# A decoder kernel with nine row slots instead of ten, a resident weight block, and h turned by TensorE

## The chip, the core and the metric

The kernel runs on one core of one Trainium2 chip. The metric is the device time in microseconds, the median of several runs of the same program. The neighbouring cores do nothing.

## What is computed

A decoder trunk of two layers on 256 tokens of width 1024, all in 32-bit floats. Cut to what matters here:

```python
for l in range(2):                                   # DEPTH
    z = rmsnorm(x, g_mix[l]) @ w_in[l]               # zq, the keys and values, conv, pooling inputs
    x = x + concat([nsa(z), conv(z), pool(z)]) @ w_out[l]
    x = x + cross_attention(rmsnorm(x, g_xa[l]), rmsnorm(mem, g_mem[l]), ...)
    x = x + peer(rmsnorm(x, g_ffn[l]), ...)          # the experts
out = rmsnorm(x, final_g)

def peer(h, wq, sub_keys, u, v):                     # 8 heads x 16 experts of 16384 for each token
    expert_idx, gate = top16_of_pairs(top16(h @ wq, sub_keys))
    act = gelu(einsum('cd,chkd->chk', h, u[expert_idx]))
    return einsum('chk,chkd->cd', gate * act, v[expert_idx])
```

For each of the 256 tokens and in each layer, 128 experts are chosen by the data, and a row of `u` and one of `v` (1024 numbers each) are fetched for each of them.

`_pool_mixer` subtracts each value from its mean over the last 2, 4, 8 or 16 tokens.

## The kernel before

The tokens are worked on in two tiles of 128, one token in each partition. With two layers that makes four pieces of dense work (attention, convolution, pooling, cross-attention, choice of experts) and four pieces of experts' work. The program has five stages. Stage 0 does the dense work of layer 0, tile 0 alone. Stages 1 to 3 each do the experts' work of the piece before and the dense work of the next piece side by side. The last stage does the experts' work of the last piece and the final norm. A barrier of all engines stands between stages. In the profiled execution the stages start at 228.2, 655.6, 1060.3 and 1470.2 us; the prediction calls the one from 228 the second stage, the one from 655 the third and the one from 1060 the fourth.

**The experts' work.** 128 rows are gathered one after the other; "row" k is, for each of the 128 tokens, its k-th expert's `u` and `v`, 8 KB a partition. GpSimd issues the gathers (line 499) into `uv_rows`, which has `ROWS` slots, ten before (`ROWS = AHEAD * B` with `AHEAD` 5 and `B` 2). Before a gather it waits until TensorE has released the slot's last user (`slots_free`). After the gather it spreads the row's gate into a diagonal `diag` (line 493). VectorE takes the dot of the row's `u` half with h, held in PSUM as `h_ps` (line 540). ScalarE takes the gelu of two dots at a time (line 993) and multiplies it into `diag` (line 999). TensorE multiplies `diag` with the `v` half and adds into `acc_pe` (line 1265), and with that releases the slot. At the start of a stage VectorE copies `h_ffn` to `h_ps` (line 545). `h_ffn` is x times gain times 1/rms, made at line 845 in the step `ffn_norm`; the gain of 512 KB is loaded by SyncE for each stage (line 462).

**The dense work.** Each engine runs through the same written list of steps (`PLAN`, `MEM_PLAN`, `FIRST_PLAN`, `LAST_PLAN`). Between steps `run` lets it do as many pairs of rows as the table `TURNS` says, worked out once by `spread` from the steps' written lengths. So each engine's order is fixed, and an engine that waits in one step does none of the pairs behind it. The first steps of a stage are `mix_norm` (the norm on ScalarE and VectorE, then TensorE turns x) and `zq`, the first of the products with a weight block. VectorE has two dots ahead of the small instructions of `mix_norm`.

**The weight blocks.** The weights come in blocks of 16 KB a partition (2048 KB). SyncE loads them in the order of use into `w_ring`, which has two places (`RING`), and waits before each load until the last product with the block that holds the place is done. In stage 0 the slots of `uv_rows` are still empty, and three more places lie in them: ten slots minus the four that hold the memory tokens. `FIRST_PLACES` is the table of places of stage 0. Block `zq` of a layer is used in both of its tiles and is loaded in each.

**The rest.** `tcon` holds constants of a tile; its parts `cur` and `prev` are the pooling matrices, 4 x 128 columns each, multiplied in TensorE's step `turn_kv`. `h_t` holds the turned and gained activations that the products read.

Of the kernel before, what the change touches and what calls it, by code (L numbers as in the profile page):

```python
# [11 lines left out]
ALU = mybir.AluOpType  # L12
# [3 lines left out]
P = 128  # L16
# [24 lines left out]
B = 2  # L41
# [3 lines left out]
ROWS = AHEAD * B  # L45
# [21 lines left out]
for _name, _w in (("causal", S), ("cadd", NC), ("cvalid", NC), ("cur", 4 * P), ("prev", 4 * P), ("flag", 1)):  # L67
    TC[_name] = (_n, _w)
    _n += _w
# [37 lines left out]
FIRST_PLACES = [2, 3, 4, 0, 1] * 3 + [2, 0, 1, 0, 1]  # L107
# [79 lines left out]
for _bits in (10, 20):  # L187
# [6 lines left out]
    "tile_consts_loaded", "smalls_loaded", "fixed_loaded", "ident_loaded", "mem_loaded", "ffn_gain_loaded",  # L194
# [18 lines left out]
def build_program(nc, a):  # L213
    with ExitStack() as ctx:
# [8 lines left out]
        w_ring = sb("w_ring", [P, RING, KC * BLK])  # L223
        mem_k = sb("mem_k", [P, KC, N_MEM])
# [14 lines left out]
        pt_cmp = sb("pt_cmp", [P, P])  # L239
        h_ffn = sb("h_ffn", [P, D])  # L240
        hc = sb("hc", [P, 2, HIST + P])
        conv = sb("conv", [P, 2, P])
        conv_u = sb("conv_u", [P, 2, P])
        conv_e = sb("conv_e", [P, 2, P])
# [45 lines left out]
        junk = h_t[:, :, :].rearrange("p c t -> p (c t)")  # L290
# [20 lines left out]
        def stage(dense, experts, mem_layer=None, first=False, last=False):  # L311
# [9 lines left out]
            blocks = [b for job in jobs for b in JOB_BLOCKS.get(job, ())]  # L321
            at = {n: i for i, n in enumerate(jobs)}
            places = FIRST_PLACES if first else [i % RING for i in range(len(blocks))]
# [45 lines left out]
            def place_rows(name):  # L369

                if place[name] < RING:
                    return w_ring[:, place[name], :]
# [45 lines left out]
            with nc.Block(no_gpsimd_drain=not last) as block:  # L418

                @block.sync  # L420
                def _(sp):
# [37 lines left out]
                    def load_gain(source):  # L459
                        if experts is not None:  # L460
                            sp.wait_ge(sems["h_taken"], 1)
                        sp.dma_start(h_ffn[:, :], source).then_inc(sems["ffn_gain_loaded"], 16)

                    for i, name in enumerate(blocks):
# [12 lines left out]
                        if i == (4 if first else 1):  # L477
                            if first:
                                sp.dma_start(xs[:, D:2 * D], a["x"][:, 1, :]).then_inc(sems["x_later_loaded"], 16)
                            load_gain(a["ffn_gain"][bass.ds(layer, 1), :, :].rearrange("a p n -> (a p) n"))  # L480
                    if last:
                        load_gain(a["final_gain"])
# [49 lines left out]
                def _(dve):  # L532
# [111 lines left out]
                    def conv_in():  # L644

                        dve.wait_ge(sems["tile_consts_loaded"], 16)
                        if first:
# [6 lines left out]
                                              conv_e[:, :, :], ALU.mult)  # L654
# [1073 lines left out]
```

## Time and profile before

| | |
|---|---|
| median of 3 runs | 1790.23 us (1786.97 to 1796.47) |
| the profiled execution | 1803.4 us, its span 1801.6 us |
| busy: TensorE, VectorE, GpSimd, ScalarE | 1334.3, 1111.0, 663.8, 490.4 us |
| DMA | 701.66 MB, mean 389 GB/s; 536.90 MB of it are gathered rows |
| GpSimd waits for TensorE before a gather | 844.6 us |
| VectorE waits for a row before a dot | 262.1 us |
| mean granted TensorE clock | 0.864 |

The busy times are of one profiled execution, counted from its first instruction to its last. A share of busy time says little here, since the engines take turns at being the one that is waited for. The table by stretches in the section of rows gives, for a stretch of time, how long each engine was busy, and in its last two columns the busy share of the 16 DMA engines (1.00 is all of the time) and the rate. In a timeline the number in square brackets is the time that the engine stood idle before the row, and behind the arrow what ended it.

### The profile page before, as it was taken

Reading aid. Unit: us, or ns where it says so; the run is one execution under the profiler, and the core shown is the slowest. Engines: PE = TensorE matmul, PEld = TensorE weight load, DVE = VectorE, ACT = ScalarE, POOL = GpSimd, SP = SyncE. Lnnn points to the kernel's source line nnn. Section 1 sums busy time; section 2 is a strip of 40 time slices with the busy share of each in tenths; the row PEclk is TensorE's granted clock in tenths of the full one; section 3 lists DMA queues with packets and bytes.
Section 4 is the critical chain, followed back from the end, with each engine's and each line's share of the span. In section 5 each row is a group of like instructions: output and inputs, shape, how many; then the busy total and the mean of one; then the engine's idle time right before and its main releaser. Section 6 shows DMA issues by size and latency. Waiting matters only on the chain. (4 is left out here: it accounts for less than half of the span.)

```text
span 1801.6 us, 22636 instructions
## 1 busy us (share of the span) xinstructions
PE 1334.3 (74%) x8260; PEld 681.1 (38%) x8260; DVE 1111.0 (62%) x2763; ACT 490.4 (27%) x1290; POOL 663.8 (37%) x1028
## 2 busy tenths in 40 slices
PE   7999876669999847667778757667878656565554
PEld 5856742235564523222364433223454421111110
DVE  5510588895343757798444767798434758954444
ACT  3411132253212222225222222226322212211111
POOL 0000224344333433345333434444424344465551
PEclk9999988689999979878989979888989876787777
DMA  9742699999999999999999999999999989999996
GB/s 391 291 174 87 275 395 423 392 397 417 424 423 422 422 396 422 422 413 421 424 421 422 420 416 423 420 405 421 422 423 422 421 360 421 403 407 421 421 421 258
DMA packets 87519, 701.66 MB, mean 389 GB/s; under 512 B 10097, under 2 KB 10225, under 8 KB 12145
## 3 DMA queue, kind: packets, MB, share of 16 engines
q0 software_dynamic: 73728, 536.90, 72.0%
q1 hardware_dynamic: 13680, 163.32, 22.0%
q8 instruction: 65, 1.06, 0.2%
q14 instruction: 46, 0.37, 0.1%
HBM read 698.09 MB, written 2.10 MB: 389 GB/s over the span
## 5 line engine op out<-in xcount | busy, mean ns | idle before, releaser
L499 POOL DMA_INDIRECT uv_rows<-uv_in,idx x512 | 504.3, 985 | 1087.7 <-PE acc_pe L1265 844.6
L1265 PE MATMUL acc_pe<-uv_rows,diag 64*64 64x512 f32 x4096 | 614.9, 729 | 346.5 <-ACT diag L999 331.5
L540 DVE CUSTOM_DVE_ANT_0 uv_rows<-uv_rows,h_ps 128x1024 f32<-128x1024 f32 x512 | 609.1, 1218 | 267.9 <-DMA uv_rows<-uv_in,idx 262.1
L1265 PEld LDWEIGHTS acc_pe<-uv_rows,diag 64*64 64x64 f32 x4096 | 154.0, 153 | 719.8 <-ACT diag L999 505.0
L993 ACT ACTIVATE gelu_b<-act_b 128x2 f32<-128x2 f32 x256 | 52.2, 204 | 783.6 <-DVE act_b L540 771.2
L1292 PE MATMUL bank<-w_ring,h_t 128*128 128x512 f32 x400 | 189.0, 628 | 17.9 <-DMA w_ring<-blocks_in 12.3
L1292 PEld LDWEIGHTS bank<-h_t,w_ring 128*128 128x128 f32 x1600 | 182.1, 193 | 20.7 <-issue 18.1
L1292 PE MATMUL bank<-h_t,w_ring 128*128 128x128 f32 x1600 | 186.4, 278 | 2.2 <-DMA w_ring<-blocks_in 1.2
L493 POOL TENSOR_TENSOR diag<-ident_st,gate 128x64 f32<-128x64 f32 x512 | 159.3, 312 | 14.7 <-DVE gate L933 5.2
L999 ACT ACTIVATE diag<-diag,gelu_b 128x64 f32<-128x64 f32 x512 | 151.2, 342 | 8.6 <-ACT gelu_b L993 0.2
L1292 PEld LDWEIGHTS bank<-w_ring,h_t 128*128 128x128 f32 x400 | 78.4, 201 | 129.2 <-issue 104.7
L1037 ACT ACTIVATE area<-bank 128x512 f32<-128x512 f32 (+1 forms) x73 | 42.3, 579 | 257.2 <-PE bank L1292 221.6
L812 DVE TENSOR_TENSOR xs<-xs,bank 128x512 f32<-128x512 f32 x16 | 11.0, 687 | 156.0 <-PE bank L1292 156.0
L1287 PE MATMUL bank<-ident,area 128*128 128x128 f32 x208 | 34.9, 324 | 51.1 <-ACT area L1012 40.7
L666 DVE SCALAR_TENSOR_TENSOR conv<-hc,smalls,conv 128x128 f32<-128x128 f32 x240 | 68.8, 357 | 0.4
L1287 PEld LDWEIGHTS bank<-ident,area 128*128 128x128 f32 x208 | 28.8, 168 | 69.1 <-ACT area L1012 34.9
L993 ACT ACT_TABLE_LOAD x39 | 50.0, 1283 | 1.7
L540 DVE DVE_READ_ACCUMULATOR2_ANT act_b<- 128x1 f32 x512 | 42.0, 82 | 0.0
L852 DVE MAX8 half_v<-area 128x8 f32<-128x128 f32 x128 | 28.0, 279 | 18.9 <-ACTq L1040 18.6
L572 DVE TENSOR_TENSOR h_t<-bank,smalls 128x512 f32<-128x512 f32 x24 | 15.8, 688 | 34.6 <-PE bank L1287 26.0
L855 DVE FIND_INDEX8 half_i<-half_v,area 128x8 uint32<-128x128 f32 x128 | 34.1, 283 | 0.0
L1292 PE MATMUL bank<-uv_rows 128*128 128x256 f32 (+1 forms) x96 | 29.1, 460 | 1.0 <-DVE h_t L572 1.0
(204 smaller groups left out, 1137.2 us busy)
## 6 DMA issues: line engine op xcount, KB each, us to landing
w_ring<-blocks_in SPq DMA_DIRECT2D x62, 2048.0 KB
uv_rows<-blocks_in SPq DMA_DIRECT2D x9, 2048.0 KB, 15.1
uv_rows<-uv_in,idx POOLq DMA_INDIRECT x512
tcon<-tile_consts_in SPq DMA_DIRECT2D x4, 656.5 KB, 10.5
uv_rows<-blocks_in SPq DMA_DIRECT2D x2, 1024.0 KB, 8.5
h_ffn<-ffn_gain_in SPq DMA_DIRECT2D x4, 512.0 KB, 28.5
xs<-x_in SPq DMA_DIRECT2D x2, 512.0 KB, 17.2
uv_rows<-mem_in SPq DMA_DIRECT2D x1, 1024.0 KB, 14.8
```

The costliest lines, as they stand in the source:

```text
L493: nc.gpsimd.tensor_tensor(diag[:, slot_of(k), :], ident_st[:, :], gate[:, k:k + 1].to_broadcast([P, HT]), ALU.mult).then_inc(sems["gates_s ...
L499: nc.gpsimd.indirect_dma_start(uv_rows[:, slot_of(k), :, :].rearrange("p a n -> p (a n)"), None, a["uv"], bass.IndirectOffsetOnAxis(ap=idx ...
L540: v.tensor_tensor_reduce(u_row, u_row, h_ps[:, :], 1.0, 0.0, ALU.mult, ALU.add, act_b[:, k // B % AHEAD, k % B:k % B + 1]).then_inc(sems[" ...
L666: ins = v.scalar_tensor_tensor(out=conv[:, g, :], in0=hc[:, g, k:k + P], scalar=small("cw", g * CONV_W + k, 1), in1=conv[:, g, :], op0=ALU ...
L852: step.mark(v.max(top[:, g, lo], values(g)))
L855: step.mark(v.max_index(where[:, g, lo], top[:, g, lo], values(g)))
L993: s.activation(gelu_b[:, b % AHEAD, :], act_b[:, b % AHEAD, :], ACT.Gelu_apprx_tanh).then_inc(sems["gelu_done"], 1)
L999: s.activation(diag[:, slot_of(k), :], diag[:, slot_of(k), :], ACT.Copy, scale=gelu_b[:, b % AHEAD, k % B:k % B + 1]).then_inc(sems["diag_ ...
L1037: drain(s.activation(out, src, func, **kw), job)
L1265: mm = pe.matmul(acc_pe[c * HT:(c + 1) * HT, r * BLK:(r + 1) * BLK], diag[tok, slot_of(k), :], uv_rows[tok, slot_of(k), 1, c * BLK:(c + 1) ...
L1287: mm = pe.transpose(out[:, i * P:(i + 1) * P], src, ident[:, :])
L1292: mm = pe.matmul(out, lhs, rhs, start=(i == 0), stop=(i == len(pairs) - 1))
```

## The change

1. `ROWS` is 9. The slots of `uv_rows` are 0 to 8, and so is `diag`.
2. A buffer `kept` of 16 KB a partition holds the block `zq`. It is loaded in the first of a layer's tiles and not in the second. The other blocks take the two places of the ring in turn without it. In stage 0 the kept block stands beside four places, two of them in slots 4 to 7.
3. h is no longer made by VectorE in `ffn_norm`. At the start of a stage TensorE turns `h_t` (x times gain) back into `h_ps` with eight transposes; VectorE copies 1/rms into `h_scale`, and the gelu multiplies its input by it. The gain is no longer loaded as rows; the final gain is loaded into `area2`.
4. The pooling matrix for the tokens before the tile has 16 columns instead of 128, since no later token reaches back that far.
5. `pt_cmp`, `conv_u`, `conv_e` and the squares of the norm move into areas that exist already.

```diff
-ROWS = AHEAD * B
+ROWS = 9
-for _name, _w in (("causal", S), ..., ("prev", 4 * P), ("flag", 1)):
+for _name, _w in (("causal", S), ..., ("prev", 4 * NC), ("flag", 1)):
+KEPT = "zq"
+KEPT_PLACE = 4
-FIRST_PLACES = [2, 3, 4, 0, 1] * 3 + [2, 0, 1, 0, 1]
+FIRST_PLACES = [KEPT_PLACE] + [2, 3, 0, 1] * 3 + [2, 3, 0, 1, 0, 1, 0]
...
+            kept_earlier = dense is not None and not own_half
+            blocks = [b for job in jobs for b in JOB_BLOCKS.get(job, ()) if not (kept_earlier and b == KEPT)]
+            in_ring = [b for b in blocks if b != KEPT]
+            places = FIRST_PLACES if first else [KEPT_PLACE if b == KEPT else in_ring.index(b) % RING for b in blocks]
...
                     def experts_start():
-                        v.tensor_copy(h_ps[:, :], h_ffn[:, :]).then_inc(sems["h_taken"], 1)
+                        step(v.tensor_copy(h_scale[:, :], st[:, 3:4]))
                         dve.wait_ge(sems["h_taken"], 1)
...
-                        dve.wait_ge(sems["ffn_gain_loaded"], 16)
-                        dve.wait_ge(sems["norm_rstd"], norms[0])
-                        step(v.scalar_tensor_tensor(out=h_ffn[:, :], in0=xs[:, tile * D:(tile + 1) * D],
-                                                    scalar=st[:, 3:4], in1=h_ffn[:, :], op0=ALU.mult, op1=ALU.mult))
...
                             s.activation(gelu_b[:, b % AHEAD, :], act_b[:, b % AHEAD, :],
-                                         ACT.Gelu_apprx_tanh).then_inc(sems["gelu_done"], 1)
+                                         ACT.Gelu_apprx_tanh, scale=h_scale[:, 0:1]).then_inc(
+                                             sems["gelu_done"], 1)
...
                     def need_weights(name):
-                        pe.wait_ge(w_landed[place[name]], 16 * use[name])
+                        if name in place:
+                            pe.wait_ge(w_landed[place[name]], 16 * use[name])
...
+                    def start():
+                        if experts is not None:
+                            for c in range(KC):
+                                mm = pe.transpose(h_ps[:, c * P:(c + 1) * P], h_t[:, c, :], ident[:, :])
+                            mm.then_inc(sems["h_taken"], 1)
```

On SyncE's queue, whose rows are the loads, the stages from 655 and from 1060 stand like this before, from the small weights of the one to the last block of the other:

```order
L432 DMA smalls<-smalls_in 128x1633
L423 DMA tcon<-tile_consts_in 128x1313
L436 DMA w_ring<-blocks_in 128x4096 x2
L462 DMA h_ffn<-ffn_gain_in 128x1024
L436 DMA w_ring<-blocks_in 128x4096 x14
L418 UNCONDITIONAL_BRANCH
L420 UNCONDITIONAL_BRANCH
L423 DMA tcon<-tile_consts_in 128x1313
L436 DMA w_ring<-blocks_in 128x4096 x2
L462 DMA h_ffn<-ffn_gain_in 128x1024
L436 DMA w_ring<-blocks_in 128x4096 x14
```

And the same place on SyncE's queue now:

```order
L439 DMA smalls<-smalls_in 128x1633
L430 DMA tcon<-tile_consts_in 128x865
L443 DMA kept<-blocks_in 128x4096
L443 DMA w_ring<-blocks_in 128x4096 x15
L425 UNCONDITIONAL_BRANCH
L427 UNCONDITIONAL_BRANCH
L430 DMA tcon<-tile_consts_in 128x865
L443 DMA w_ring<-blocks_in 128x4096 x15
```

The gain is gone from both, zq goes to its own buffer in the first and is gone from the second, and the constants are narrower.

On TensorE the first rows of the stage from 228 (turn of x, pair of rows, zq's product, pair, product ab) are before:

```order
L1287 MATMUL bank<-ident,area 128x128 x8
L1265 MATMUL acc_pe<-uv_rows,diag 64x512 x8
L1292 MATMUL bank<-w_ring,h_t 128x512 x8
L1265 MATMUL acc_pe<-uv_rows,diag 64x512 x8
L1292 MATMUL bank<-h_t,w_ring 128x128 x32
```

And now:

```order
L1576 MATMUL h_ps<-ident,h_t 128x128 x8
L1285 MATMUL bank<-ident,area 128x128 x8
L1262 MATMUL acc_pe<-uv_rows,diag 64x512 x8
L1290 MATMUL bank<-kept,h_t 128x512 x8
L1262 MATMUL acc_pe<-uv_rows,diag 64x512 x8
L1290 MATMUL bank<-h_t,w_ring 128x128 x32
```

Eight transposes stand ahead of everything, and zq's product reads `kept`.

On VectorE the same stage begins before with the copy of h, two dots (two rows each) and the small instructions of the norm:

```order
L545 COPY h_ps<-h_ffn 128x1024
L540 ISA uv_rows,act_b<-uv_rows,h_ps 128x1024
L540 ISA act_b 128x1
L540 ISA uv_rows,act_b<-uv_rows,h_ps 128x1024
L540 ISA act_b 128x1
L564 TENSOR_SCALAR st<-st 128x1
```

And now:

```order
L545 COPY h_scale<-st 128x1
L540 ISA uv_rows,act_b<-uv_rows,h_ps 128x1024
L540 ISA act_b 128x1
L540 ISA uv_rows,act_b<-uv_rows,h_ps 128x1024
L540 ISA act_b 128x1
L564 TENSOR_SCALAR st<-st 128x1
```

The copy has one column, and the first dot behind it waits for TensorE's transposes.

## Rows read from the trace of the kernel before

**Rows 1.** Ten stretches (us, length, busy by engine, clock, DMA share, GB/s).
```profile
225.00:247.00 22.00, 13.18 (x44) 6.28 (x43) 15.72 (x52) 7.28 (x12) 2.55 (x4) 0.61 1.01 423
...
247.00:251.00 4.00, 3.33 (x8) 1.14 (x6) 3.90 (x13) 0.60 (x1) 0.00 (x0) 1.00 0.78 322
...
334.00:339.00 5.00, 5.00 (x60) 2.24 (x52) 5.00 (x14) 0.80 (x3) 0.00 (x0) 0.61 0.71 293
...
406.00:572.00 166.00, 158.96 (x863) 88.64 (x864) 67.83 (x119) 40.98 (x110) 60.82 (x95) 0.99 1.01 421
...
636.00:642.00 6.00, 6.00 (x52) 3.86 (x55) 2.94 (x6) 2.09 (x5) 1.79 (x3) 1.00 0.80 298
...
783.00:787.00 4.00, 4.00 (x48) 1.71 (x44) 4.00 (x9) 1.08 (x5) 0.00 (x0) 0.75 0.94 391
...
1043.00:1047.00 4.00, 4.00 (x36) 1.86 (x39) 2.16 (x4) 2.28 (x7) 2.07 (x3) 1.00 0.99 393
...
1180.00:1189.00 9.00, 7.49 (x84) 2.98 (x88) 8.75 (x23) 1.61 (x7) 2.80 (x4) 0.76 0.96 372
...
1489.00:1581.00 92.00, 56.88 (x298) 12.98 (x296) 82.58 (x225) 23.52 (x66) 45.99 (x71) 0.69 1.00 407
...
1581.00:1776.00 195.00, 112.23 (x652) 26.04 (x640) 97.17 (x160) 31.54 (x120) 100.24 (x158) 0.77 1.01 420
```

**Rows 2.** Timeline of GpSimd: gathers, with the idle time before.
```profile
947.63 0.97 POOL L499 DMA_INDIRECT uv_rows<-uv_in,idx  x1 [13.42 <-PE acc_pe L1265]
...
956.57 0.97 POOL L499 DMA_INDIRECT uv_rows<-uv_in,idx  x1 [6.19 <-PE acc_pe L1265]
...
1351.71 0.98 POOL L499 DMA_INDIRECT uv_rows<-uv_in,idx  x1 [9.24 <-PE acc_pe L1265]
```

**Rows 3.** DMA issues: count, KB each, median us to landing.
```profile
w_ring<-blocks_in SPq DMA_DIRECT2D x62, 2048.0 KB
...
tcon<-tile_consts_in SPq DMA_DIRECT2D x4, 656.5 KB, 10.5
...
h_ffn<-ffn_gain_in SPq DMA_DIRECT2D x4, 512.0 KB, 28.5
```

**Rows 4.** Timeline of TensorE: start, us, count, idle before.
```profile
202.36 7.41 PE L1292 MATMUL bank<-h_t,w_ring 128*128 128x128 f32 x64 [1.18 <-DMA w_ring<-blocks_in]
...
240.78 9.56 PE L1292 MATMUL bank<-w_ring,h_t 128*128 128x512 f32 x16 [0.70 <-DMA w_ring<-blocks_in]
...
675.87 8.76 PE L1292 MATMUL bank<-w_ring,h_t 128*128 128x512 f32 x16 [6.61 <-DMA w_ring<-blocks_in]
...
1065.71 1.97 PE L1287 MATMUL bank<-ident,area 128*128 128x128 f32 x8 [11.74 <-ACT area L1012]
...
1077.04 9.56 PE L1292 MATMUL bank<-w_ring,h_t 128*128 128x512 f32 x16 [5.02 <-DMA w_ring<-blocks_in]
```

**Rows 5.** Timeline of VectorE at the fourth stage's start.
```profile
1060.34 1.23 DVE L545 COPY h_ps<-h_ffn 128x1024 f32<-128x1024 f32 x1 [3.47 <-PEq L1611]
...
1096.93 1.22 DVE L540 CUSTOM_DVE_ANT_0 uv_rows<-uv_rows,h_ps 128x1024 f32<-128x1024 f32 x1 [4.28 <-DMA uv_rows<-uv_in,idx]
```

**Rows 6.** Chain that ended last, one piece: start us, us, what.
```profile
1638.84 21.00 DMA uv_rows<-uv_in,idx
```

**Rows 7.** Waits of VectorE for rows, 290 to 330, then 830 to 945.
```profile
DVE uv_rows L540 <- DMA uv_rows<-uv_in,idx: 3.9, 3, 1.5
...
DVE uv_rows L540 <- DMA uv_rows<-uv_in,idx: 23.1, 14, 5.6
```

**Rows 8.** Groups of instructions by form: count, busy us, mean ns.
```profile
L1037 ACT ACTIVATE area<-bank 128x512 f32<-128x512 f32 x67 | 40.0, 598 | 250.9 <-PE bank L1292 215.3 <-remote 14.0 <-PE bank L1313 11.2
...
L1037 ACT ACTIVATE area<-bank,st 128x512 f32<-128x512 f32 x15 | 10.3, 684 | 14.9 <-PE bank L1292 14.9
...
L993 ACT ACTIVATE gelu_b<-act_b 128x2 f32<-128x2 f32 x256 | 52.2, 204 | 783.6 <-DVE act_b L540 771.2 <-issue 7.7
...
L1292 PE MATMUL bank<-tcon,pool_prev 128*64 128x128 f32 x32 | 3.3, 273 | 0.0
```

More of the change, by code:

```diff
@@ L66 @@
 _n = 0
-for _name, _w in (("causal", S), ("cadd", NC), ("cvalid", NC), ("cur", 4 * P), ("prev", 4 * P), ("flag", 1)):
+for _name, _w in (("causal", S), ("cadd", NC), ("cvalid", NC), ("cur", 4 * P), ("prev", 4 * NC), ("flag", 1)):
     TC[_name] = (_n, _w)
@@ L223, in build_program @@
         w_ring = sb("w_ring", [P, RING, KC * BLK])
+        kept = sb("kept", [P, KC * BLK])
         mem_k = sb("mem_k", [P, KC, N_MEM])
@@ L238, in build_program @@
         p_cmp = sb("p_cmp", [P, HEADS, NC])
-        pt_cmp = sb("pt_cmp", [P, P])
-        h_ffn = sb("h_ffn", [P, D])
+        h_scale = sb("h_scale", [P, 1])
         hc = sb("hc", [P, 2, HIST + P])
         conv = sb("conv", [P, 2, P])
-        conv_u = sb("conv_u", [P, 2, P])
-        conv_e = sb("conv_e", [P, 2, P])
         smalls = sb("smalls", [P, N_SMALL])
@@ L289, in build_program @@
         o_sum, o_one = area3[:, 1024:1536], area3[:, 1536:2048]
-        junk = h_t[:, :, :].rearrange("p c t -> p (c t)")
+        conv_e = area2[:, 1664:1920].rearrange("p (g t) -> p g t", g=2)
+        conv_u = area3[:, 512:768].rearrange("p (g t) -> p g t", g=2)
+        pt_cmp = area3[:, 768:896]
+        final_gain, junk = area2[:, 0:D], area2[:, D:2 * D]
         cat_t = h_t
@@ L369, in place_rows @@
             def place_rows(name):
+                if name == KEPT:
+                    return kept[:, :]
                 if place[name] < RING:
@@ L476, in _ @@
                         load_block(name)
[L477 to L480, printed above, removed]
+                        if first and i == 4:
+                            sp.dma_start(xs[:, D:2 * D], a["x"][:, 1, :]).then_inc(sems["x_later_loaded"], 16)
                     if last:
-                        load_gain(a["final_gain"])
+                        sp.dma_start(final_gain, a["final_gain"]).then_inc(sems["final_gain_loaded"], 16)
                         for t in range(TILES):
@@ L980, in _ @@
                             step(v.reciprocal(st[:, 3:4], st[:, 2:3]))
-                            v.scalar_tensor_tensor(out=rows, in0=rows, scalar=st[:, 3:4], in1=h_ffn[:, :],
+                            v.scalar_tensor_tensor(out=rows, in0=rows, scalar=st[:, 3:4], in1=final_gain,
                                                    op0=ALU.mult, op1=ALU.mult).then_inc(sems["out_ready"], 1)
@@ L1021, in tile_norm @@
                     def tile_norm():
-                        norm(xs[:, tile * D:(tile + 1) * D], x_n, junk)
+                        norm(xs[:, tile * D:(tile + 1) * D], x_n, x_n)
                     def tile_rstd():
@@ L1648, in constants @@
         put(tile, "cur", cur.reshape(P, -1))
-        put(tile, "prev", prev.reshape(P, -1))
+        put(tile, "prev", prev[:, :, :NC].reshape(P, -1))
         put(tile, "flag", float(tile > 0))
```

30 lines of the change are left out of this document (12 added, 18 removed).

## The prediction, made before the result was known

> **What bounds the kernel now.** I read the profile in this order: the busy time by stretches, the waits of GpSimd and VectorE, then single stretches of the timeline at the stage starts. In the table by stretches [rows 1] the reader is to look at the last two columns. In the long stretches from 225, 406 and 1581 the DMA engines move 420 to 423 GB/s with a share of 1.01: they are full. One gathered row of experts is 128 x 8 KB = 1.049 MB, so at 421 GB/s it costs 2.49 us. In six short ones the figure falls to between 293 and 393: all ten slots have landed, nothing is queued, and the DMA waits for TensorE to give a slot back. So the time is neither all DMA nor all compute. It is a relay: the DMA runs dry, compute holds the baton, then VectorE stands waiting for a row, and the DMA holds it again. From 406 to 572 TensorE is busy for 159 of 166 us and holds it alone; from 1489 to 1581 VectorE is busy for 82.6 of 92. From 1581 to 1776 it is the DMA.
>
> The gathers of GpSimd show how near to dry the queue comes where the share does not fall [rows 2]: before 947.63 GpSimd waited 13.42 us for TensorE, issued two gathers, and waited 6.19 us more. In those 22 us the DMA moves the worth of 9 rows. The gather at 1351.71 follows on 9.24 us of the same wait, and I read the place around 1356 in the same way.
>
> **The bytes that go.** Twice a block zq (2048 KB), four times the gain of 512 KB, and of each of four tile constants 656.5 x 448/1313 = 224 KB [rows 3]. The copies of the first stage (736 KB) fall into a stretch that TensorE fills, and I cost them at nothing. The rest is 2 x 2048 + 3 x 736 = 6304 KB = 6.46 MB, at 421 GB/s **15.3 us**. It is worth that only where the DMA holds the baton afterwards.
> - Second stage (from 228): 2784 KB, 6.8 us. Up to 247 the DMA moves 423 GB/s, then it runs dry by itself (322 GB/s over 247 to 251) [rows 1]. Without the block it runs dry sooner and no row is issued earlier. TensorE waits 0.70 us for zq here [rows 4], and that is what can be had. I take 0.
> - Third stage (from 655): 736 KB, 1.8 us. zq must still be loaded, and TensorE keeps its wait of 6.61 us [rows 4]. A third block, zk1, is now queued right behind instead of after zq's product, which slows the rows of that moment and speeds those after. I take 0.9 us.
> - Fourth stage (from 1060): 2784 KB, 6.8 us. TensorE waits 5.02 us for zq [rows 4] while VectorE waits 4.28 us for the next row [rows 5]. Both go together: 5.0 us.
> Taken: **-5.9 us**; bounds 0 and -15.3.
>
> By the Trainium skill ("DMA: Bandwidth & Descriptors", Where 436 GB/s comes from) a transfer from HBM is bound at about 358 GB/s a core, where the rows show 421 to 423 with the neighbour idle; by the page's figure the same bytes would be 18.0 us, and the measurement decides.
>
> **The slot that goes.** While the DMA holds the baton a tenth slot is of no use: after 1581 a row takes 21.00 us to come [rows 6], so 21.00 / 2.49 = 8 rows are queued at a time. It is of use each time the queue runs dry. With ten slots the DMA has then put ten rows ahead; with nine it stops one row sooner and restarts at the same event, so the row that VectorE later waits for comes 2.49 us later. The price is due if VectorE does wait for a row before the next dry place, by 2.49 us or more. I count the dry places at 247, 636, 783, 953, 1043, 1180, 1356 and in 1489 to 1581 [rows 1, 2]. Behind them VectorE waits for rows: 3.9 us between 290 and 330, 23.1 between 830 and 945 [rows 7], and so behind each of the others. The place at 334 I leave out, since TensorE's full stretch from 406 follows. Those at 636 and 1043 lie just ahead of a stage's end, where VectorE stands 3.47 us at the barrier anyway [rows 5]; I count the two as one. Seven places x 2.49 = **+17.4 us**. Bounds: 0, if the landed rows that TensorE has not yet used cover for the missing one, and 9 x 2.49 = 22.4. In the first stage there are four places in the ring instead of five beside the kept block. Each block is still issued tens of us ahead of its product. The one load that TensorE waits for, before 202.36 [rows 4], is released by the same product as before. I take 0, bounds 0 and +5.
>
> **The turn of h.** Before, a stage opens with one copy of 1.23 us on VectorE and then the first dot [rows 5]. Now it opens with eight transposes on TensorE. Eight such transposes took 1.97 us at 1065.71 [rows 4], in a stretch with TensorE just started; with a handover on either side I take 2.2 us. VectorE's tiny copy hides beside them. The first dot is some 0.9 us later, and as the norm's small steps stand behind the first two dots in VectorE's order, so is the whole stage. Four stages; in the third VectorE waits for the small weights afterwards anyway, so 3 x 0.9 = **+2.7 us**. Bounds 0 and 4 x 1.5 = +6. The product h x gain x 1/rms that goes (four instructions of VectorE) stood under TensorE's products for the queries, so nothing is gained.
>
> **The gelu's scale.** A scale from memory is read per partition. No such gelu is in the trace. The nearest rows are the same copy of 128x512 with and without such a scale: 684 against 598 ns [rows 8]. So +86 ns on each of 256 gelus of 204 ns. ScalarE waits most of the time, so in the sum I put it at 0. If it stood on the path each time it would be 256 x 0.086 = +22 us, and below 0 nothing speaks for it.
>
> The Trainium skill ("ScalarE: Activation LUTs", What ACT_TABLE_LOAD costs) says that each per-partition pointer operand adds about 93 ns; the rows here agree in size with 86. By that rule, used on all 256 gelus, ScalarE has 24 us more work, and it is a rule against this change.
>
> **Edits at nothing.** The 32 products against pool_prev shrink from 128 to 16 columns; all 32 together are 3.3 us on TensorE [rows 8], within its stretches of waiting, bound -2. The areas that conv_e, conv_u, pt_cmp and the final gain now share add no wait beyond those there are.
>
> **Sum.** -5.9 + 17.4 + 2.7 = +14.2 us. On the profiled execution's 1803.4 us (span 1801.6 and 1.8 around it) that is 1817.6. That execution is 13.2 us above the median of the runs, 1790.2; as the terms are waits and bytes that do not depend on this, I put the same 14.2 on the median: **1804 us**.
>
> **The rivals.**
> 1. The bytes decide, faster. The DMA share is 1.01 nearly everywhere, and rows that have landed stand unused in the compute-bound stretches, so a ninth slot would be as good as a tenth. Then -15.3 + 2.7 = -12.6, 1778 us. Against it: the stretches at 298 and 322 GB/s show that ten slots are not enough already. It decides if the lost bytes count in full and the slot at under 3 us.
> 2. They cancel. About half of the dry places cost their 2.49 us, because TensorE rather than VectorE ends the stretch behind them (as from 406 to 572), so +8.7, and the bytes give 8 as the fourth stage's start is worth all its 6.8: +3.4 with the turn of h, 1794 us; 1781 to 1799 counts as this case.
> 3. The gelu's scale stands on the path. In the slot's round (dot, gelu, diag, product, gather) it adds 86 ns, which matters where the queue is dry, above all from 1489 on. With all of it, +22 on top of 14.2: 1826 us. Against it: VectorE, not ScalarE, is the busy one there.
>
> **How the numbers follow.** I give the forecast 0.51, rival 1 0.17, rival 2 0.27, rival 3 0.05. The forecast's own range is 1797 to 1816. What a measurement of this kernel can tell from no change is 0.5%, 9 us, so faster means under 1781 and slower over 1799. Rival 1 is faster: 0.17. Rival 2 is within, and so is a little of the forecast: 0.30. The rest is slower: 0.53. The range of 8 in 10 reaches from rival 1's time to above the forecast's own: 1778 to 1818.
>
> **What would show it.** The table by stretches should show the same dry places, each longer by 2 to 3 us, above all at the transition near 1581, and GpSimd's waits for TensorE should grow. TensorE's wait for zq should be gone in the fourth stage and stay in the third. The first dot should start about 2.2 us after a stage's barrier instead of 1.3. The first gather should stay at 201. I am wrong if VectorE's total wait for rows falls, or if the stretches between dry places shorten by the bytes and the dry ones do not grow.

## The result and the profile after

| | before | after |
|---|---|---|
| median of the runs | 1791.32 us (1786.97 to 1796.47) | 1820.26 us (1816.38 to 1826.61) |
| ratio, 95% interval | 1 | 1.0153 [1.0128, 1.0178] |
| the profiled execution, its span | 1803.4, 1801.6 us | 1816.38, 1814.6 us |
| DMA | 701.66 MB, mean 389 GB/s | 694.45 MB, mean 383 GB/s |
| GpSimd waits for TensorE before a gather | 844.6 us | 872.3 us |
| VectorE waits for a row | 262.1 us | 283.9 us |

The changed kernel is slower by 29 us; the forecast was 14 us slower, with a range that ended at 1818. Its stages start at 220.3, 650.4, 1070.7 and 1481.1 us. The table by stretches of the changed kernel, for the places that answer to [rows 1]:

```profile
225.00:247.00 22.00, 19.06 (x93) 10.35 (x94) 19.57 (x69) 5.88 (x15) 5.11 (x8) 0.83 1.01 410
247.00:251.00 4.00, 4.00 (x37) 3.35 (x39) 3.88 (x8) 0.29 (x1) 0.00 (x0) 1.00 0.78 305
324.00:330.00 6.00, 6.00 (x68) 2.57 (x64) 5.97 (x15) 1.81 (x7) 0.00 (x0) 0.66 0.45 184
400.00:560.00 160.00, 153.34 (x816) 84.33 (x812) 63.38 (x108) 37.10 (x97) 56.94 (x88) 0.99 1.01 423
626.00:638.00 12.00, 10.32 (x91) 5.04 (x89) 5.23 (x9) 3.94 (x11) 1.55 (x3) 1.00 0.32 124
774.00:784.00 10.00, 7.94 (x88) 3.13 (x92) 9.75 (x25) 2.15 (x7) 2.64 (x4) 0.77 0.88 326
1045.00:1058.00 13.00, 10.66 (x92) 5.06 (x90) 6.18 (x10) 3.93 (x11) 1.28 (x2) 1.00 0.37 154
1183.00:1193.00 10.00, 7.77 (x85) 2.98 (x89) 9.75 (x25) 2.12 (x7) 2.63 (x4) 0.74 0.90 333
1454.00:1470.00 16.00, 11.17 (x96) 5.57 (x95) 7.66 (x12) 3.93 (x11) 2.69 (x5) 1.00 0.42 157
1498.00:1592.00 94.00, 53.99 (x296) 12.79 (x300) 84.26 (x233) 25.15 (x66) 45.76 (x71) 0.75 0.99 399
1592.00:1790.00 198.00, 117.46 (x652) 26.79 (x644) 98.07 (x161) 35.27 (x120) 102.01 (x160) 0.73 1.01 419
```

The dry places are where they were. A stretch of length t at a lower rate loses t x (1 - rate/421) us of DMA time. By that the places at 324, 774 and 1183 lose 1 to 2 us more than their counterparts at 334, 783 and 1180. Three stand out, at 626, 1045 and 1454: 12 to 16 us long with 124 to 157 GB/s, which loses 8 to 10 us each. Each ends 11 to 13 us ahead of a stage's barrier. What stands there shows in the timeline of GpSimd at the third of these, in the kernel before (the first and the last of the ten gathers for the next stage):

```profile
1454.59 0.98 POOL L499 DMA_INDIRECT uv_rows<-uv_in,idx  x1 [9.93 <-PE acc_pe L1265]
...
1467.71 0.97 POOL L499 DMA_INDIRECT uv_rows<-uv_in,idx  x1 [0.16 <-issue]
```

and in the changed kernel (the last gather of this stage, then the first, second and ninth for the next):

```profile
1448.76 0.97 POOL L499 DMA_INDIRECT uv_rows<-uv_in,idx  x1 [0.22 <-PE acc_pe L1262]
...
1466.96 0.97 POOL L499 DMA_INDIRECT uv_rows<-uv_in,idx  x1 [16.90 <-PE acc_pe L1262]
...
1468.41 0.97 POOL L499 DMA_INDIRECT uv_rows<-uv_in,idx  x1 [0.16 <-issue]
...
1478.59 0.97 POOL L499 DMA_INDIRECT uv_rows<-uv_in,idx  x1 [0.16 <-issue]
```

GpSimd waits 16.90 us in place of 9.93 before it may fetch the first row of the next stage. Then it issues all nine in a row, one per 1.45 us, and is through at 1479.9. VectorE had added the experts' sums by 1469.9 and stands at the barrier, which GpSimd holds, until 1481.08. The waits of VectorE at the starts of the four stages with experts' work, before and then after (us in total, times, longest):

```profile
DVE h_ps L545 <- PEq L1611: 22.1, 4, 9.4
```

```profile
DVE h_scale L545 <- PEq L1617: 42.5, 4, 11.2
```

That is 20.4 us more, nearly all of it at the last three starts (4.6, 3.5 and 4.6 us before, 11.2 each after). It can't be set against the 29 directly, since the two profiled executions are only 13.0 us apart (spans 1801.6 and 1814.6): the profiled execution of the kernel before (1803.4 us) is slower than all the runs that its median is taken of, and its stage 0 ends at 228.2 where that of the changed kernel ends at 220.3. The experiments below settle what the wait costs.

**Why nine slots make GpSimd wait longer.** In every stage row k takes slot k mod `ROWS`, and the first rows of the next stage begin at slot 0 again. The line that orders them is, in both kernels, line 526: row k of the next stage waits for the last of the 128 rows that uses its slot.

```python
pool.wait_ge(sems["slots_free"], max(range(k, PAIRS, ROWS)) + 1)
```

With ten slots, slot 0 was last used by row 120, and the next seven rows wait for rows 121 to 127 in turn (the last two, for rows 118 and 119, stand behind them). With nine slots, 128 mod 9 is 2: slot 0 was last used by row 126. So row 0 of the next stage waits for row 126, row 1 for the very last, row 127, and rows 2 to 8, whose slots (rows 119 to 125) come free one after the other before that, stand behind them on GpSimd's queue. The stream of rows is cut at each of three stage ends: it starts again only when all that had landed, but for the last row, is used up.

### The profile page after: what moved, and what is told of

The parts are those of the page before. It is cut to its first block and busy times, and to the rows that moved or that the text cites. A ratio compares the mean times of both kernels' runs of the same rounds, so it can differ in the third digit from the quotient of the medians.

```text
span 1814.6 us, 22682 instructions
## 1 busy us (share of the span) xinstructions
PE 1346.9 (74%) x8292; PEld 685.8 (38%) x8292; DVE 1102.6 (61%) x2759; ACT 512.3 (28%) x1290; POOL 662.8 (37%) x1028
## 2 busy tenths in 40 slices
DMA packets 86654, 694.45 MB, mean 383 GB/s; under 512 B 10000, under 2 KB 10128, under 8 KB 11536
## 3 DMA queue, kind: packets, MB, share of 16 engines
q8 instruction: 65, 1.06, 0.2%
## 5 line engine op out<-in xcount | busy, mean ns | idle before, releaser
L499 POOL DMA_INDIRECT uv_rows<-uv_in,idx x512 | 503.8, 984 | 1110.7 <-PE acc_pe L1262 872.3
L1262 PE MATMUL acc_pe<-uv_rows,diag 64*64 64x512 f32 x4096 | 628.8, 743 | 337.6 <-ACT diag L996 327.7
L540 DVE CUSTOM_DVE_ANT_0 uv_rows<-uv_rows,h_ps 128x1024 f32<-128x1024 f32 x512 | 609.5, 1217 | 295.4 <-DMA uv_rows<-uv_in,idx 283.9
L989 ACT ACTIVATE gelu_b<-act_b,h_scale 128x2 f32<-128x2 f32 x256 | 75.4, 294 | 786.7 <-DVE act_b L540 782.0
L1290 PEld LDWEIGHTS bank<-h_t,w_ring 128*128 128x128 f32 x1728 | 195.5, 192 | 21.2 <-issue 18.3
L1290 PE MATMUL bank<-h_t,w_ring 128*128 128x128 f32 x1728 | 199.9, 277 | 2.4 <-DMA w_ring<-blocks_in 1.5
L1290 PE MATMUL bank<-w_ring,h_t 128*128 128x512 f32 x336 | 152.0, 606 | 4.8 <-ACTq L1037 4.8
L1034 ACT ACTIVATE area<-bank 128x512 f32<-128x512 f32 (+2 forms) x77 | 43.2, 560 | 238.7 <-PE bank L1290 219.6
L1290 PEld LDWEIGHTS bank<-w_ring,h_t 128*128 128x128 f32 x336 | 63.3, 193 | 94.9 <-issue 88.6
L1285 PE MATMUL bank<-ident,area 128*128 128x128 f32 x216 | 34.6, 310 | 28.2 <-ACT area L1009 20.4
L1576 PE MATMUL h_ps<-ident,h_t 128*128 128x128 f32 x32 | 6.9, 386 | 44.1 <-PEq L1617 44.1
## 6 DMA issues: line engine op xcount, KB each, us to landing
tcon<-tile_consts_in SPq DMA_DIRECT2D x4, 432.5 KB, 10.4
uv_rows<-mem_in SPq DMA_DIRECT2D x1, 1024.0 KB, 14.6
```

The source lines that it names most:

```text
L499: nc.gpsimd.indirect_dma_start(uv_rows[:, slot_of(k), :, :].rearrange("p a n -> p (a n)"), None, a["uv"], bass.IndirectOffsetOnAxis(ap=idx ...
L540: v.tensor_tensor_reduce(u_row, u_row, h_ps[:, :], 1.0, 0.0, ALU.mult, ALU.add, act_b[:, k // B % AHEAD, k % B:k % B + 1]).then_inc(sems[" ...
L989: s.activation(gelu_b[:, b % AHEAD, :], act_b[:, b % AHEAD, :], ACT.Gelu_apprx_tanh, scale=h_scale[:, 0:1]).then_inc(sems["gelu_done"], 1)
L1034: drain(s.activation(out, src, func, **kw), job)
L1262: mm = pe.matmul(acc_pe[c * HT:(c + 1) * HT, r * BLK:(r + 1) * BLK], diag[tok, slot_of(k), :], uv_rows[tok, slot_of(k), 1, c * BLK:(c + 1) ...
L1285: mm = pe.transpose(out[:, i * P:(i + 1) * P], src, ident[:, :])
```

## The experiments

Ratios are to the kernel before, run on the same chip, with the 95% interval. "Ahead of the barriers" is the mean rate of the DMA over the last 25 us before the stages' starts (three starts, where full is 421 GB/s). In the kernel before this rate is 363 GB/s, and in the changed kernel 251.

| label | what it is | ratio | GB/s ahead of the barriers |
|---|---|---|---|
| e1 | the changed kernel again | 1.0167 [1.0144, 1.0190] | |
| e2 | ten slots, zq through the ring | 0.9986 [0.9971, 1.0000] | 381 |
| e3 | nine slots, zq through the ring | 1.0193 [1.0171, 1.0214] | 247 |
| e4 | changed, gelu without scale | 1.0130 [1.0105, 1.0155] | |
| e5 | eight slots | 1.0225 [1.0205, 1.0245] | 357 |
| e6 | seven slots | 1.0524 [1.0500, 1.0548] | 240 |
| e7 | eleven slots | 0.9970 [0.9956, 0.9984] | 352 |
| e8 | ten, VectorE scales h in PSUM | 1.0004 [0.9991, 1.0016] | |
| e9 | ten, rows one by one | 1.0026 [1.0013, 1.0038] | 359 |
| e10 | nine, rows one by one | 1.0225 [1.0205, 1.0244] | 250 |
| e11 | ten, half of zq kept | 0.9964 [0.9951, 0.9976] | 361 |
| e12 | ten, gelu without scale | 0.9987 [0.9974, 1.0000] | |
| e13 | e3, slots numbered on | 1.0049 [1.0033, 1.0066] | 394 |
| e14 | e2, slots begin at that of row 126 | 1.0119 [1.0090, 1.0147] | 259 |
| e15 | changed, slots numbered on | 0.9999 [0.9981, 1.0016] | 420 |
| e16 | e11, slots numbered on | 0.9909 [0.9880, 0.9937] | 421 |
| e17 | e6, slots numbered on | 1.0442 [1.0420, 1.0465] | 360 |
| e18 | e7, slots numbered on | 0.9933 [0.9914, 0.9951] | 421 |

**The parts apart: e1, e2, e3.** e2 has everything of the change but two things: it has ten slots, and zq is loaded in each tile (with the places of stage 0 as before). e3 is e2 with nine slots; the fifth place of stage 0 then lies in `kept`. The edits, against the changed kernel:

```diff
-ROWS = 9
+ROWS = 10      # e2 alone
...
-KEPT = "zq"
+KEPT = None
...
-FIRST_PLACES = [KEPT_PLACE] + [2, 3, 0, 1] * 3 + [2, 3, 0, 1, 0, 1, 0]
+FIRST_PLACES = [2, 3, 4, 0, 1] * 3 + [2, 0, 1, 0, 1]
```

> The changed kernel once more, as the base for the three beside it. Theory A (the lost slot costs 2.5 us at each dry place of the DMA, and there are more dry places than I counted): ratio to the kernel before 1.015, that is +25 to +30 us. Theory B (the first trace of it happened to be a good one and the first trace of the kernel before a bad one; the stage from 650 to 1070, +15.6 us there, is the typical loss): the same ratio, and this second trace shows a loss of over 5 us in more than that one stage. Each stage's length is what I will compare.

> Ten slots again and zq loaded for both tiles through the ring of two places as before; the other parts of the change stay (h turned by TensorE, 1/rms in the gelu, no gain loads, the pooling matrix of 16 columns). Theory A: all of the loss is in the pair slot and kept block, so this is at the kernel before or a little under it: 1788 to 1796 us, since the lost gain loads are worth 2 to 4 us and the later first dot costs 3. Rival (the gelu's per-partition scale and the later start carry the loss): 1805 to 1820 us.

> Nine slots, and zq streamed as before; stage 0 keeps its five places, the fifth in the buffer that the change adds. Against the ten-slot kernel beside it only the slot differs. Theory A: 20 to 35 us slower than that one, and 0 to 10 us slower than the changed kernel, which saves the bytes of zq. Prediction's step: +17.4 us for the slot. Rival (the slot costs little, under 8 us, and the kept block's other loads are in the way): within 8 us of the ten-slot kernel.

e1 repeats the result. e3 against e2 is the slot alone: 1.0193 against 0.9986, **37 us** (2.07% of 1791), a little above the 20 to 35 us that I had expected. I had costed it at 17.4 in the prediction. Keeping zq, e3 to e1, gives back 5.7 us by the medians (1827.57 to 1821.86) and 4.7 by the ratios; the intervals of the two overlap, so this is known only to some 5 us either way. What is left of the change (turn of h, scale, narrow constants, the gain no longer loaded) is e2 itself: -2.5 us, at the edge of the noise.

The lengths of the stages in the profiled executions, stage 0 first:

| | stage 0 | from about 220 | from 650 | from 1060 | from 1470 |
|---|---|---|---|---|---|
| before | 228.2 | 427.4 | 404.7 | 409.9 | 331.4 |
| changed | 220.3 | 430.1 | 420.3 | 410.4 | 333.5 |
| e1, changed again | 219.7 | 434.0 | 419.0 | 412.8 | 332.2 |
| e2, ten slots | 219.5 | 426.4 | 411.8 | 403.1 | 332.3 |
| e3, nine slots | 218.1 | 436.0 | 422.2 | 415.3 | 334.0 |

A stage of the same kernel differs by up to 4 us between two executions (changed and e1). From e2 to e3 the three stages that end at a barrier with gathers ahead of it grow by 9.6, 10.4 and 12.2 us, and the last one, which has no such end, by 1.7.

**How many slots: e5, e6, e7.** `ROWS` is 8, 7 and 11 (`AHEAD` is 6 for 11). My theory at this point was that the rows are handed out in pairs and that an odd slot has no partner.

> The nine-slot kernel with zq streamed (1.0193 of the kernel before, ten slots being 0.9986, so the tenth slot is worth 37 us) with one slot fewer still. Theory A (each slot costs one row's time, 2.5 us, at each dry place, and there are some 15 such places): 9 to 8 costs as much as 10 to 9 or more, 35 to 50 us, 1.04 or above. Theory P (rows are worked in pairs: the ninth slot holds a row whose partner has no slot, so nine slots run four pairs ahead as eight do, where ten run five ahead): 9 to 8 costs under 15 us, 1.020 to 1.027.

> Seven slots, zq streamed, stage 0 with its five places (two of them in extra buffers). Theory A: from eight another 40 to 60 us. Theory P: seven run three pairs ahead, so this step is the large one again, 50 to 90 us below eight slots and at least three times the step from nine to eight.

> Eleven slots, zq streamed, the rings of dots and gelus of six pairs instead of five; otherwise the ten-slot kernel at 0.9986. Theory A: a slot is worth one row at each dry place, less than the tenth, 10 to 25 us faster than ten slots, 0.985 to 0.993. Theory P: the eleventh slot has no partner, within 8 us of ten slots, 0.994 to 1.000.

The price of a slot is uneven: 11 to 10 0.2%, 10 to 9 2.1%, 9 to 8 0.3%, 8 to 7 3.0%. No price of one row's time per dry place gives that. The theory of the pairs seemed to.

**Without pairs: e9, e10.**

```diff
-B = 2
+B = 1
-AHEAD = 5
+AHEAD = 10
```

`LAG`, `AT_START` and the turns of the last stage are doubled with it, so that the steps have as many rows between them.

> Ten slots, zq streamed, but rows worked one by one: each engine's list hands out single rows between the dense steps, and ScalarE takes a gelu for each row. More gelus (512 instead of 256) and other places of the rows between the steps, so its level against the paired kernel (0.9986) is open: 0.99 to 1.02. It is the base for the nine-slot kernel beside it.

> The same with nine slots. Theory P (nine slots lose a whole pair, because rows are handed out in pairs): with single rows the ninth slot is of full use and only one row is lost at each dry place, so 10 to 9 costs half of the 37 us of the paired kernels, 10 to 24 us. Theory A (the slot itself is worth 37 us): again 30 us or more.

Nine single rows lose 2.0% to ten, as the pairs did. The theory of the pairs fell here. The column on the right of the table above is what led on: the rate ahead of the barriers is 240 to 250 GB/s with seven and nine slots and 352 to 381 with eight, ten and eleven. 128 mod 7 is 2, as 128 mod 9 is; with 8, 10 and 11 slots the first row waits for row 120, 120 and 121.

**The order of the waits: e13 and e14.** In e13 and in e15 to e18 the slots are numbered on through the stages. `turn` counts the pieces of experts' work, and `last_in` gives the last row of this stage in a slot. In e14 the shift is 126 a stage, with ten slots. Cut to the lines that matter:

```diff
+SHIFT = 128     # 126 in e14
...
-            def slot_of(k):
-                return k % ROWS
+            turn = -1 if experts is None else experts
+
+            def slot_of(k, stage_at=None):
+                return ((turn if stage_at is None else stage_at) * SHIFT + k) % ROWS
...
-                            pool.wait_ge(sems["slots_free"], max(range(k, PAIRS, ROWS)) + 1)
-                            gather(k)
-                            spread_gate(k)
+                            pool.wait_ge(sems["slots_free"], last_in(slot_of(k, turn + 1)) + 1)
+                            gather(k, turn + 1)
+                            spread_gate(k, turn + 1)
```

> nine_streamed with one thing changed: the slots are numbered on through the stages (slot = (128 x stage + row) mod 9) and no longer begin at slot 0 in each stage. Before, row 0 of the next stage wants slot 0, whose last user among 128 rows is row 126; row 1 wants that of row 127; rows 2 to 8 want those of rows 119 to 125 but stand behind on GpSimd's queue. With ten slots (128 mod 10 = 8) row 0 wants the slot of row 120. Theory H (the order of the wait): the 9-slot loss sits mostly there; in the profile after GpSimd waits 16.90 us before 1466.96 and then issues nine gathers in a row of 1.45 us each. The wait then moves from row 126 to row 119, the three stage ends lose some 7 us less each, so 3 x 7 = 21 us: ratio to before 1.0075, about 1807 us. Theory S (a ninth row is simply too few to bridge the dry place): nothing changes, 1.019.

> ten_streamed, ten slots, but the slots of a next stage begin at that of row 126 (slot = (126 x stage + row) mod 10), so that the first row of a stage waits for row 126 to be done, as it does with nine. The number of slots, the bytes and the work are those of ten_streamed (ratio 0.9986). Theory H: it falls back to nearly where nine_streamed stands, +15 to +24 us, ratio 1.007 to 1.012. Theory S: 0.9986.

Both came out on the side of theory H (the order of the wait), and they are each other's converse. Nine slots numbered on gain 1.44%, 26 us, on e3; ten slots that must wait for row 126 lose 1.33%, 24 us, with not a slot, byte or row's work more or less. e13 gained more than the 21 us expected. The stretches of 25 us ahead of the three barriers, first in the kernel before, then in the changed kernel, in e13 and in e14:

```profile
630.60:655.60 25.00, 16.12 (x141) 10.54 (x139) 9.81 (x16) 4.37 (x12) 12.78 (x20) 0.93 0.94 373
1035.30:1060.30 25.00, 16.14 (x140) 10.34 (x136) 11.34 (x18) 4.47 (x14) 12.79 (x20) 0.96 1.00 406
1445.20:1470.20 25.00, 15.84 (x140) 10.44 (x136) 8.40 (x15) 3.60 (x13) 12.79 (x20) 0.88 0.79 311
```

```profile
625.40:650.40 25.00, 10.93 (x97) 5.68 (x95) 6.47 (x13) 3.96 (x12) 11.52 (x18) 0.77 0.66 252
1045.70:1070.70 25.00, 9.96 (x86) 4.37 (x85) 7.25 (x12) 3.94 (x12) 11.51 (x18) 0.83 0.66 256
1456.10:1481.10 25.00, 9.08 (x79) 3.52 (x77) 7.24 (x13) 3.97 (x12) 11.51 (x18) 0.81 0.63 245
```

```profile
624.20:649.20 25.00, 18.49 (x161) 11.88 (x161) 12.23 (x21) 6.34 (x19) 13.16 (x22) 0.95 0.95 379
1034.00:1059.00 25.00, 19.35 (x169) 11.85 (x161) 11.36 (x19) 5.95 (x18) 15.31 (x24) 0.95 1.02 421
1443.80:1468.80 25.00, 19.24 (x168) 11.92 (x161) 11.06 (x18) 5.97 (x18) 15.34 (x24) 0.94 0.97 381
```

```profile
630.20:655.20 25.00, 9.47 (x84) 4.22 (x83) 6.47 (x11) 4.00 (x12) 12.80 (x20) 0.75 0.69 266
1044.60:1069.60 25.00, 7.78 (x68) 2.75 (x61) 6.43 (x10) 3.35 (x11) 12.79 (x20) 0.79 0.67 262
1456.10:1481.10 25.00, 9.48 (x84) 4.24 (x83) 6.47 (x11) 4.00 (x12) 12.79 (x20) 0.75 0.64 248
```

The reader is to look at the last column. The DMA time that is lost in such a stretch is 25 x (1 - rate/421). It sums to 30.9 us in e3 (its three rates are 257, 235 and 250) and 4.9 in e13: 26.0 less, where the ratios say 26. It is 7.1 in e2 and 28.9 in e14: 21.8 more, where they say 24. In the timeline of GpSimd in e13 the rows of the next stage go out as slots come free, the first at once behind this stage's last, the second after 6.47 us:

```profile
1448.32 0.97 POOL L506 DMA_INDIRECT uv_rows<-uv_in,idx  x1 [0.16 <-issue]
...
1456.09 0.97 POOL L506 DMA_INDIRECT uv_rows<-uv_in,idx  x1 [6.47 <-PE acc_pe L1269]
```

In e14 it is held for 16.33 us, as in the changed kernel with nine:

```profile
1465.49 0.97 POOL L503 DMA_INDIRECT uv_rows<-uv_in,idx  x1 [16.33 <-PE acc_pe L1266]
```

VectorE's waits at the starts of stages follow. In e3, e13 and e2 they are, in this order:

```profile
DVE h_scale L545 <- PEq L1617: 42.3, 4, 11.2
```

```profile
DVE h_scale L552 <- PEq L1624: 17.2, 4, 8.7
```

```profile
DVE h_scale L542 <- PEq L1614: 23.9, 4, 7.8
```

In e14 they are 45.7 us. That is 25.1 us less from e3 to e13 and 21.8 more from e2 to e14, again close to the 26 and 24 of the ratios. Two things happen at once here: the rows come later, and the barrier waits for the late gathers. Every run that moves the first gather moves both, so how the loss divides between them is not shown.

**The changed kernel and the others, numbered on: e15 to e18.**

> The changed kernel with the slots numbered on through the stages, nothing else. Theory H: 1.0153 less 21 of 1790, so 1.0036, about 1799 us; the waits of GpSimd ahead of the three barriers fall from some 17 to under 10 us. Theory S: 1.0153 to 1.0167 as it is.

> seven_streamed (ratio 1.0524) with the slots numbered on through the stages. 128 mod 7 = 2, so with seven slots, too, the first row of a stage waits for row 126; with eight (128 mod 8 = 0) it waits for row 120 anyway, and numbering on would change nothing there. Theory H: three stage ends get back 7 to 8 us each, as with nine: 1.0524 less 0.012 to 0.014, so 1.038 to 1.040, and the seventh slot's own price beside eight (1.0225) is then 1.6% in place of 3.0%. Theory S: 1.052.

> eleven_streamed (ratio 0.997) with the slots numbered on. 128 mod 11 = 7: row 0 of a stage wants the slot of row 121, while those of rows 117 to 120 are free before; numbered on it is issued four rows earlier. In e16 two rows earlier were worth 0.55% (0.9964 to 0.9909). Theory H: 0.990 to 0.993. Theory S: 0.997.

The changed kernel with this alone is level with the one before, 0.9999 [0.9981, 1.0016]; that is 28 us gained on its first measurement, more than the 21 that I had expected. Its three stretches ahead of the barriers show 418, 420 and 421 GB/s; the one ahead of the last start:

```profile
1429.80:1454.80 25.00, 19.22 (x169) 11.91 (x161) 11.36 (x19) 5.95 (x18) 15.29 (x24) 0.95 1.01 421
```

VectorE's wait at the barriers fell from 42.5 to 17.2 us:

```profile
DVE h_scale L552 <- PEq L1624: 17.2, 4, 8.6
```

e17 gained 0.8% where 1.2 to 1.4 was expected: the direction holds, the size is less, and seven slots are simply few. e18 gained 0.37% and ended just outside the range that I gave.

With the order of the waits put right the price of a slot is no longer uneven (with eight slots, 128 mod 8 = 0, numbering on changes nothing, so e5 stands for it): from nine to eight 1.8%, 31 us (e13 and e5), from eight to seven 2.2%, 39 us (e5 and e17), from eleven to nine 1.2% for the two, some 10 us each (e18 and e13). So the small step from nine to eight in the first series (0.3%) was two effects against each other: one slot fewer, and no wait for row 126.

**The best version: e11 and e16.** Ten slots leave 8 KB a partition, room for half of zq. In e11 a layer's second tile loads only the other half into the ring; e16 numbers the slots on as well.

```diff
+        zq_half = sb("zq_half", [P, 4 * BLK])
...
+                            if own_half:
+                                sp.dma_start(zq_half[:, :], block_of("zq", 0, 2 * D)).then_inc(
+                                    sems["zq_half_loaded"], 16)
+                            sp.dma_start(place_rows("zq")[:, 2 * D:4 * D], block_of("zq", 2 * D, 2 * D)).then_inc(
+                                w_landed[place["zq"]], 16)
```

> Ten slots and the first half of zq (1024 KB) kept for a layer's second tile, which fits into the space that the change frees without giving up a slot. The whole block with one place fewer in stage 0 was worth 5.7 us in the nine-slot kernels. Half of it: 2 to 4 us under the ten-slot kernel, 0.9965 to 0.9975 of the kernel before. If TensorE's wait for the second half stays as long as for the whole block: no gain, 0.9986.

> The best version so far (ten slots, half of zq kept, ratio 0.9964) with the slots numbered on. With ten slots rows 8 and 9 of the next stage have had free slots (those of rows 118 and 119) since before, but stand behind rows 0 to 7; numbered on, the first two gathers go out two rows earlier. Theory H: two rows earlier at three stage ends, up to 2 x 2.49 us each where the DMA loses 3.4 us at the first two ends now and nothing at the third: -3 to -7 us, ratio 0.9925 to 0.995. Theory S: 0.9964.

e16 takes 1777.95 us, 0.9909 [0.9880, 0.9937]: faster than both kernels, some 42 us under the changed one. It gained more than expected (0.9925 to 0.995), as its rate ahead of the barriers rose from 361 to 421 GB/s at all three: 10.7 us of DMA time, and the ratio fell by 0.55%, 10 us.

**The gelu's scale: e4, e12, e8.** e4 and e12 leave the multiplication by 1/rms out, so that their gelu takes an input of another size; nothing else changes.

```diff
-                                         ACT.Gelu_apprx_tanh, scale=h_scale[:, 0:1]).then_inc(
+                                         ACT.Gelu_apprx_tanh).then_inc(
```

> The changed kernel with the gelu taken without the per-partition scale; 1/rms is left out of the dots. Theory A: the scale adds 90 ns to each of 256 gelus, but beside other work, so under 4 us faster than the changed kernel, 1816 to 1820 us. Rival 3 of the prediction (the scale stands on the slot's round): 10 to 22 us faster, 1798 to 1810 us.

> The ten-slot kernel with the gelu taken without the scale from memory; 1/rms is left out of the dots. With nine slots this gave 6.4 us. If the scale lengthens the slot's round and costs only where slots are short: 0 to 3 us with ten. If it costs on ScalarE's path whatever the slots: 6 us again, 0.995.

> The ten-slot kernel with h scaled by 1/rms in place on VectorE after TensorE's turn, so the gelu has no scale from memory. In the nine-slot kernel the scale cost 6 us (1.0167 against 1.013). If that holds with ten slots: minus 6, plus at most 4 x 1.23 for the scaling at the stage starts, so 1785 to 1792 us, 0.994 to 0.998. If the scale only costs where slots are short: no gain, 0.998 to 1.002.

With nine slots the scale costs 1.0167 - 1.0130, 6.6 us; the intervals overlap, against the first measurement of the changed kernel (1.0153) it is 4 us, and it lies between what theory A and rival 3 wanted. With ten nothing is seen (0.9986 and 0.9987). In e8 VectorE scales h in PSUM once a stage instead: 0.18% above e2, with overlapping intervals, so no gain over the scale in the gelu, and a loss of 3 us is not shown. Why the scale costs something with nine slots, if it does, was not settled: I did not run the plain gelu with the slots numbered on, which would tell whether it sits in the same three places.

## Why the prediction failed, step by step

**The slot: the term that was mis-sized.** I put 17.4 us; it is 37. The sum was seven places at 2.49 us, six of them inside stages and one for the stage ends. By e2 and e3, the DMA time lost in the 25 us ahead of the barriers grows by 30.9 - 7.1 = 23.8 us, and the rest, 37 - 23.8 = 13 us, is left for the six other places, at 2.2 us each. A second pair says the same: e3 and e14 both wait for row 126 and differ in the slot, by 0.74%, 13 us. So the price of one row per dry place was near the truth inside the stages for this step (that it is no general price, the 31 us from nine slots to eight show), and the stage ends were wrong by a factor of ten. The list of dry places also lacked the third stage end, where the kernel before moves 311 GB/s over the last 25 us before 1470.2, and the place at 334, which I had left out, lost about 2 us of DMA time more. The sentence that failed is "Those at 636 and 1043 lie just ahead of a stage's end, where VectorE stands 3.47 us at the barrier anyway; I count the two as one", and beneath it the premise that with nine slots the queue "stops one row sooner and restarts at the same event". At a stage's end it restarts at another event: when row 126 is done, not row 120. I took the rule of slots for a ring with one place less, and it is a ring only within a stage. This could be had before any run, from line 526 and the numbers 128, 9 and 10. I also read the 3.47 us at the barrier as slack. It is the time in which GpSimd issues its last gathers, so whatever delays the first of them delays the barrier by as much.

**The bytes: the signs right, the size not shown.** I predicted -5.9 for zq, the gain and the constants together, of which 0.9 was for a stage where only gain and constants go. Measured for zq alone is some -5, uncertain by about as much (e3 to e1); the gain and the constants are in e2's -2.5 us, beside the turn of h. All that is not the slot was -5.9 + 2.7 = -3.2 in the sum, and is -2.5 - 5.7 = -8.2 by the runs (-7.2 by the ratios). So these terms erred too, by 4 to 5 us and the other way. That the -5.0 lies in the fourth stage, as I wrote, can't be seen in stage lengths that scatter by 4 us. TensorE's wait for zq is gone in the fourth stage, and stays in the third, as forecast (before: [rows 4]); the timeline of TensorE after:

```profile
671.05 9.29 PE L1290 MATMUL bank<-kept,h_t 128*128 128x512 f32 x15 [6.59 <-DMA kept<-blocks_in]
...
1082.92 7.13 PE L1290 MATMUL bank<-kept,h_t 128*128 128x512 f32 x16
```

**The turn of h: the step right, its effect not to be seen.** The first dot of the fourth stage starts 2.08 us after the barrier; 2.2 was predicted, and before it was 1.26. TensorE's turn of x, too, starts 6.2 us after the barrier where it was 5.4, so the first steps of the stage do shift by the 0.8 us. VectorE, after:

```profile
1070.71 0.15 DVE L545 COPY h_scale<-st 128x1 f32<-128x1 f32 x1 [11.18 <-PEq L1617]
1072.79 1.22 DVE L540 CUSTOM_DVE_ANT_0 uv_rows<-uv_rows,h_ps 128x1024 f32<-128x1024 f32 x1 [1.93 <-PE h_ps L1576]
```

But e2, which has this too, is 2.5 us faster than the kernel before, not slower by my 2.7. The DMA is full in these microseconds (422 GB/s from 1070.7), so the 0.8 us may be hidden; that is an argument, not shown. No run took the turn alone, so the 2.5 us are not split between it and the bytes of the gain and the constants.

**The gelu's scale: the price of one right, its place not settled.** One gelu went from 204 ns [rows 8] to 294, so +90 where I took +86:

```profile
L989 ACT ACTIVATE gelu_b<-act_b,h_scale 128x2 f32<-128x2 f32 x256 | 75.4, 294 | 786.7 <-DVE act_b L540 782.0
```

The Trainium skill ("ScalarE: Activation LUTs", What ACT_TABLE_LOAD costs) gives about 93 ns for a per-partition pointer operand; the trace agrees, with 90. I put it at 0 on the path. With ten slots that holds; in the changed kernel e1 and e4 say 6.6 us, hardly clear of the noise.

**The signs that I had named.** GpSimd's waits for TensorE grew (844.6 to 872.3 us), and VectorE's for rows grew (262.1 to 283.9), as the forecast wanted. The first gather stayed where it was (201.4 us before, 199.7 after). Of the 21.8 us more that VectorE waits for rows, 9.0 lie in the second stage, 14.6 in the third and 2.7 in the last, and the fourth has 4.5 less. The growth did not lie "above all at the transition near 1581": the last stage went from 331.4 to 333.5 us, and 1498 to 1592 shows 399 GB/s. VectorE's wait for rows in the stretch that answers to the second of [rows 7] did not grow:

```profile
DVE uv_rows L540 <- DMA uv_rows<-uv_in,idx: 22.8, 14, 4.3
```

This is of 815 to 935 us, against 23.1 before. The measured parts, -2.5 (e2), +37 (the slot) and -5.7 (zq), add up to +28.8, and the result is +28.9. That they do says no more than that e1 repeats the result, since the parts are steps on the way from the kernel before to e1.

## What to carry to other kernels

A ring of buffers that is used across phases has two numbers that matter: how many places it has, and which place the next phase begins with. If each phase begins at place 0 and its length is not a multiple of the ring's size, look at which item of this phase last held the place that the next one wants first; one in-order queue makes all the others wait for it. Number the places on through the phases, and before pricing "one place less" work out the remainder for both sizes.

## What the runs showed of the hardware that I had not expected

GpSimd needs 1.45 us for a gather and its gate (0.97 and 0.30 us of work, the rest issue), so the nine that are held back to row 126 take 13 us to go out, and the barrier waits for the last. In the changed kernel the time at the end of a stage is set by this, not by VectorE, which stands idle for 11.2 us.

Eight transposes took 1.06 us at the start of the second stage and 1.94 us at that of the fourth. The granted clock tells the two apart: 1.00 (2.4 GHz) in the first case, where TensorE had stood idle for 1.92 us, and 0.50 (1.2 GHz) in the second, after 14.07 us. The rows, by stretches and then from the timeline of TensorE:

```profile
220.30:221.40 1.10, 1.06 (x8) 0.83 (x8) 0.15 (x1) 1.10 (x2) 0.00 (x0) 1.00 1.04 432
1070.70:1072.70 2.00, 1.94 (x8) 1.55 (x8) 0.15 (x1) 1.98 (x3) 0.00 (x0) 0.50 1.00 422
```

```profile
220.31 1.06 PE L1576 MATMUL h_ps<-ident,h_t 128*128 128x128 f32 x8 [1.92 <-PEq L1617]
...
1070.71 1.94 PE L1576 MATMUL h_ps<-ident,h_t 128*128 128x128 f32 x8 [14.07 <-PEq L1617]
```
